# Sliding-window attention in a hybrid decoder step: where the scores of the next head group or sample row are issued on TensorE

## The chip, the cores and the metric

One core of one Trainium2 chip runs the whole kernel. The metric is device time in microseconds (us) of one execution, the median over a few executions. The engines are named as in the profile: PE is TensorE (PEld its weight loads), DVE is VectorE, ACT is ScalarE, POOL is GpSimd and SP is SyncE, which here only issues DMAs. Each engine works through its own list of instructions in order and waits on semaphores that the others raise.

## The reference

The kernel computes one layer of a decoder for a prompt of 256 tokens and for 8 sample rows of 8 tokens each. Everything is float32. One large input projection feeds three branches (sliding-window attention, retention, a gated spatial mix), an output projection joins them, and a mixture of 32 experts follows. The change touches the attention branch only:

```
def sink_attention(q, k, v, mask, sinks):
    s = jnp.einsum('bnqhgd,bnkhd->bnhgqk', q, k) * (HEAD_DIM ** -0.5)
    s = jnp.where(mask[None, :, None, None], s, -jnp.inf)
    m = jnp.maximum(jnp.max(s, axis=-1, keepdims=True), sink)
    p = jnp.exp(s - m)
    denom = jnp.sum(p, axis=-1, keepdims=True) + jnp.exp(sink - m)
    return jnp.einsum('bnhgqk,bnkhd->bnqhgd', (p / denom).astype(v.dtype), v)
```

There are 16 query heads in 4 groups (one key and value head each), heads are 64 wide, and the window is 128. The prompt is two tiles of 128 queries: the first sees 128 keys, the second 256. Each sample row sees 128 cached keys and the 64 new ones under a mask.

## The kernel before

The order of the work on each engine is written out by hand. In the attention stage TensorE runs, for prompt tile `t` (0, 1) and head group `g` (0 to 3), this round:

1. the scores `sc` of the group, 4 heads (L1317 to L1324; one PSUM bank for tile 0, two for tile 1);
2. for the first six rounds one unit of the modulation matrix, `modulation(6 + 4t + g)` (L1216), which has nothing to do with attention;
3. two pieces of the input projection, `project(2)` (L1264 for full token tiles, L1271 for the tile of 64 sample tokens);
4. a wait until the softmax of this group is done (`probs_ready`), then the transposes `pT` of the probabilities (L1334, recorded at the helper L1200);
5. a wait until ScalarE has copied `pT` out of PSUM (L611), then the value products `pv` (L1342).

The modulation and projection are there so that TensorE has work while VectorE and ScalarE compute the softmax. For the 8 sample rows the round is the same without the modulation, with one projection piece: scores (L1354, L1355), `project(1)`, transposes, a wait for the ScalarE copies (L618, L619), value products (L1369, L1370).

VectorE adds the mask to the scores as it takes them out of PSUM into the one buffer `probs` (L859, L866, L877), does its part of the softmax (L841 to L850), and copies the value products of a prompt group out (L872) before it takes the next scores. ScalarE does the exponentials (L598), takes the projection's pieces (L548), copies the transposes, and for the sample rows takes the value products too (L622).

Small results share three PSUM banks. The list `AUX` names every use of them in the order in which TensorE issues them; entry `n` has bank `5 + n % 3`. `aux_free(name)` makes TensorE wait until entry `n - 3` has been taken out of that bank, `aux_filled` makes a reader wait for an entry, and `aux_taken` waits until one has been read.

Weights of the projections come in units of 2 MB through three slots, issued by SyncE: unit `u` is loaded when unit `u - 3` has been used up (L330). The cached keys and values of the sample rows lie in two slots. GpSimd issues the load for row `b` (L385, L386) when the value products of row `b - 2` are done. After the last row the result is transposed back (`oback`, L1377). This releases further loads by GpSimd (L402 to L409), and TensorE does one more projection piece, then waits for a layer normalisation on VectorE (L928 to L930) before the products of L1390.

Of the kernel before, what the change touches and what calls it, by code (L numbers as in the profile page):

```python
# [24 lines left out]
P = 128  # L25
# [70 lines left out]
AUX += ["ada4", "ada5", "kT0", "kT1", "kT2"]  # L96
for _t in range(2):
    AUX += [f"qT{_t}{q}" for q in range(4)]
    for _g in range(KVH):
        AUX += [f"sc{_t}{_g}{k}" for k in range(_t + 1)]  # L100
        AUX += [f"ada{6 + 4 * _t + _g}"] if 4 * _t + _g < 6 else []
        AUX += [f"pT{_t}{_g}{k}" for k in range(_t + 1)] + [f"pv{_t}{_g}"]
AUX += ["qT20", "qT21"]
for _b in range(BATCH_S):
    AUX += [f"sc2{_b}", f"pT2{_b}", f"pv2{_b}"]
AUX += ["oback0", "oback1"]
AUX += [f"mix{t}{h}" for t in range(3) for h in range(2)]
for _t in range(2):
# [17 lines left out]
def build(nc, ctx, ins, outs):  # L126
# [159 lines left out]
    def aux_bank(name):  # L286
        return ps[:, AUX_FIRST + AUX_AT[name] % AUX_BANKS, :]
# [5 lines left out]
    def aux_taken(eng, name):  # L293

        n = AUX_AT[name]
        eng.wait_ge(aux_used[n % AUX_BANKS], n // AUX_BANKS + 1)
# [899 lines left out]
    def _(pe):  # L1196
        mm = nc.tensor.matmul

        def tr(out, in_, r, **kw):
            return nc.tensor.transpose(out, in_, ident[0:r, 0:r], **kw)  # L1200

        def aux_free(name):

            n = AUX_AT[name]
            if n >= AUX_BANKS:
                pe.wait_ge(aux_used[n % AUX_BANKS], n // AUX_BANKS)
# [104 lines left out]
        softmaxes = 0  # L1311
        for t in range(3):
            aux_taken(pe, f"kT{t}")
        for t in range(2):
            transpose_queries(t)
            for g in range(KVH):
                for k in range(t + 1):  # L1317
                    name = f"sc{t}{g}{k}"
                    aux_free(name)
                    n, width = (4, P) if t == 0 else (2, 2 * P)  # L1320
                    for m in range(n):
                        last = mm(aux_bank(name)[:, m * width:(m + 1) * width], qTa[0:64, 4 * g + n * k + m, :],  # L1322
                                  kTa[0:64, g, 0:width], start=True, stop=True)
                    last.then_inc(aux_ready, 1)  # L1324
                if 4 * t + g < 6:
                    modulation(6 + 4 * t + g)
                project(2)
                softmaxes += 1
                pe.wait_ge(probs_ready, softmaxes)
                for k in range(t + 1):  # L1330
                    name = f"pT{t}{g}{k}"
                    aux_free(name)
                    for h in range(GROUP):
                        last = tr(aux_bank(name)[:, h * P:h * P + P], probs[:, h, k * P:k * P + P], P)  # L1334
                    last.then_inc(aux_ready, 1)
                name = f"pv{t}{g}"
                aux_free(name)
                for k in range(t + 1):
                    aux_taken(pe, f"pT{t}{g}{k}")
                for h in range(GROUP):  # L1340
                    for k in range(t + 1):
                        last = mm(aux_bank(name)[:, h * HD:(h + 1) * HD], pT[:, k, h * P:h * P + P],  # L1342
                                  V[:, k, 256 + g * HD:256 + (g + 1) * HD], start=(k == 0), stop=(k == t))
                last.then_inc(aux_ready, 1)

        transpose_queries(2)
        for b in range(BATCH_S):
            name = f"sc2{b}"
            aux_free(name)
            pe.wait_ge(cache_in[b % 2], 32 * (b // 2 + 1))  # L1350
            keys = cache[0:64, b % 2, 0:512].rearrange("p (h r) -> p h r", h=KVH)
            for g in range(KVH):
                q = qTs[0:64, b, GROUP * g:GROUP * (g + 1), :].rearrange("p h t -> p (h t)")
                mm(aux_bank(name)[32 * g:32 * g + 32, 0:P], q, keys[:, g, :], start=True, stop=True, skip_group_check=True)  # L1354
                last = mm(aux_bank(name)[32 * g:32 * g + 32, P:192], q, kTa[0:64, g, SEQ:TOKENS], start=True, stop=True, skip_group_check=True)  # L1355
            last.then_inc(aux_ready, 1)
            project(1)
            softmaxes += 1
            pe.wait_ge(probs_ready, softmaxes)
            name = f"pT2{b}"  # L1360
            aux_free(name)
            tr(aux_bank(name)[:, 0:P], probs[:, 0, 0:P], P)
            tr(aux_bank(name)[0:64, P:2 * P], probs[:, 0, P:192], P).then_inc(aux_ready, 1)
            name = f"pv2{b}"
            aux_free(name)
            aux_taken(pe, f"pT2{b}")
            for g in range(KVH):
                out = aux_bank(name)[0:64, 32 * g:32 * g + 32]
                mm(out, cache[:, b % 2, 512 + g * HD:512 + (g + 1) * HD], pT[:, 0, 32 * g:32 * g + 32], start=True, stop=False)  # L1369
                last = mm(out, V[0:64, 2, 256 + g * HD:256 + (g + 1) * HD], pT[0:64, 1, 32 * g:32 * g + 32], start=False, stop=True)  # L1370
            last.then_inc(aux_ready, 1)
# [379 lines left out]
```

## Time and profile before

| | us |
|---|---|
| median of 3 runs | 1659.16 (1657.5 to 1659.64) |
| profiled execution, its own time | 1667.73 |
| span of the profiled execution (first to last instruction) | 1665.9 |
| PE busy in the span | 1566.5 (94%) |
| DVE busy | 483.0 (29%) |
| ACT busy | 318.4 (19%) |
| POOL busy | 97.6 (6%) |
| mean granted TensorE clock | 0.96 of full speed |

The attention stage runs from about 112 us to about 360 us of the span. What lies after 700 us is the loop over the experts.
### The profile page before, as it was taken

How to read it: one execution, taken by the hardware profiler on the slowest of the kernel's cores; microseconds unless marked ns; L12 is line 12 of the kernel's file. 1: busy time of each engine (PE TensorE's matmuls, PEld its weight loads, DVE VectorE, ACT ScalarE, POOL GpSimd, SP SyncE). 2: the span in 40 equal slices, each digit the busy share in tenths (PEclk: the TensorE clock that was granted, in tenths of full speed). 3: DMA queues.
4: the chain of work that ended last, by engine and by line, in shares of the span. 5: the costliest groups of instructions: out<-in, count | busy, mean ns of one | idle time of the engine just before them, and what ended most of it. 6: DMA issues, size and time to landing. Idle time of an engine off the chain costs nothing.

```text
span 1665.9 us, 20091 instructions
## 1 busy us (share of the span) xinstructions
PE 1566.5 (94%) x7989; PEld 670.2 (40%) x7990; DVE 483.0 (29%) x801; ACT 318.4 (19%) x582; POOL 97.6 (6%) x102
## 2 busy tenths in 40 slices
PE   5989899979999797999999999999999999999996
PEld 4455555545455455333333333333333333333332
DVE  2141222146234735122222222222222222222224
ACT  1123321111223222111111111111111111111110
POOL 0000000120222440000000000000000000000000
PEclk8989997899999896999999999999999999999999
DMA  9563531342232561899999999999693999999993
GB/s 361 180 253 111 222 123 58 126 139 74 98 133 76 183 228 51 319 428 428 429 428 429 429 429 428 428 428 428 247 410 161 412 425 429 429 428 428 429 429 138
DMA packets 38630, 492.00 MB, mean 295 GB/s; under 512 B 4800, under 2 KB 4928, under 8 KB 9792
## 3 DMA queue, kind: packets, MB, share of 16 engines
q1 hardware_dynamic: 34144, 477.27, 69.3%
q0 software_dynamic: 4448, 14.19, 3.0%
q8 instruction: 28, 0.46, 0.1%
q14 instruction: 10, 0.08, 0.0%
HBM read 487.12 MB, written 4.33 MB: 295 GB/s over the span
## 4 chain that ended last, share of the span: by engine, by line
PE 89%; DVE 4%; DMA 3%; ACT 2%; issue 1%; POOL 1%; SPq 0%; DVEq 0%; POOLq 0%
PE ps L1593 28%; PE ps L1264 17%; PE ps L1622 14%; PE ps L1542 6%; PE ps L1556 6%; PE ps L1271 5%; PE ps L1200 4%; DMA ring<-in_w_dense 2%; PE ps L1223 1%; PE ps L1216 1%; PE ps L1598 1%; PE ps L1322 1%; PE ps L1342 1%; ACT ring L548 1%; PE ps L1504 1%
## 5 line engine op out<-in xcount | busy, mean ns | idle before, releaser
L1593 PE MATMUL ps<-ring,arena 128*64 128x512 f32 x2176 | 481.1, 595 | 2.7 <-issue 2.7
L1264 PE MATMUL ps<-ring,xT 128*128 128x512 f32 x672 | 309.6, 618 | 3.0 <-DMA ring<-in_w_dense 2.3
L1593 PEld LDWEIGHTS ps<-ring,arena 128*64 128x64 f32 x2176 | 156.2, 137 | 309.4 <-issue 306.8
L1622 PE MATMUL ps<-ring,arena 128*64 128x512 f32 x1088 | 248.5, 598 | 0.0
L1178 DVE TENSOR_TENSOR U<-ps,U 128x1024 f32<-128x1024 f32 (+1 forms) x102 | 124.4, 1220 | 248.7 <-PE ps L1556 248.7
L1264 PEld LDWEIGHTS ps<-ring,xT 128*128 128x128 f32 x672 | 130.2, 198 | 162.8 <-issue 158.4
L1622 PEld LDWEIGHTS ps<-ring,arena 128*64 128x64 f32 x1088 | 71.9, 136 | 168.2 <-issue 142.4
L1556 PE MATMUL ps<-arena 64*128 64x512 f32 x420 | 119.6, 636 | 0.8 <-ACT arena L734 0.8
L1542 PE MATMUL ps<-T,arena 128*64 128x512 f32 (+1 forms) x420 | 105.7, 621 | 1.2 <-DVE arena L1068 1.2
L1169 DVE TENSOR_SCALAR arena<-ps 128x512 f32<-128x512 f32 x34 | 23.5, 692 | 217.4 <-PE ps L1598 217.4
L707 ACT ACTIVATE W<-ps 128x512 f32<-128x512 f32 x35 | 20.9, 597 | 339.8 <-PE ps L1542 339.8
L1271 PE MATMUL ps<-ring,xT 128*64 128x256 f32 x672 | 84.1, 407 | 0.0
L1167 DVE TENSOR_SCALAR arena<-ps 128x512 f32<-128x512 f32 x34 | 23.5, 692 | 188.4 <-PE ps L1598 188.4
L1271 PEld LDWEIGHTS ps<-ring,xT 128*64 128x64 f32 x672 | 49.5, 146 | 34.1 <-issue 14.2
L725 ACT ACTIVATE arena<-arena 128x512 f32<-128x512 f32 x34 | 21.4, 629 | 205.4 <-DVE arena L1167 205.4
L548 ACT ACTIVATE ring<-ps 128x512 f32<-128x512 f32 (+1 forms) x48 | 23.4, 488 | 190.6 <-PE ps L1264 160.1
L1542 PEld LDWEIGHTS ps<-T,arena 128*64 128x64 f32 (+1 forms) x420 | 24.3, 136 | 76.9 <-issue 76.9
L731 ACT ACTIVATE arena<-ps 128x320 f32<-128x320 f32 x34 | 14.9, 437 | 203.2 <-PE ps L1556 203.2
L1200 PEld LDWEIGHTS ps<-consts,arena 128*128 128x128 f32 (+2 forms) x321 | 35.1, 138 | 41.9 <-issue 41.6
L1200 PE MATMUL ps<-consts,arena 128*128 128x128 f32 (+2 forms) x321 | 48.5, 278 | 0.5 <-ACT arena L622 0.5
L1216 PE MATMUL ps<-ring 128*32 128x128 f32 x768 | 28.3, 311 | 18.3 <-DMA ring<-in_w_dense 18.3
L1556 PEld LDWEIGHTS ps<-arena 64*128 64x128 f32 x420 | 33.6, 189 | 29.6 <-issue 29.6
(266 smaller groups left out, 1056.8 us busy)
## 6 DMA issues: line engine op xcount, KB each, us to landing
ring<-in_w_moe SPq DMA_DIRECT2D x192, 2048.0 KB, 15.1
ring<-in_w_dense SPq DMA_DIRECT2D x33, 2048.0 KB, 8.1
V<-in_state POOLq DMA_DIRECT2D x6, 256.0 KB, 9.5
out_sample_retention<-V POOLq DMA_DIRECT2D x6, 256.0 KB, 4.0
R<-in_x_prompt SPq DMA_DIRECT2D x1, 1024.0 KB, 16.7
arena<-in_cache_kT POOLq DMA_DIRECT2D x8, 128.0 KB, 3.5
arena<-in_cache_v POOLq DMA_DIRECT2D x8, 128.0 KB, 3.5
arena<-in_b_gate POOLq DMA_DIRECT2D x4, 256.0 KB, 3.7
```

Source lines behind the costliest of these rows:

```text
L548: A(buf[0:ROWS[t], t, c0 + c:c0 + c + w], src, func).then_inc(z_used, 1)
L1167: X.tensor_scalar(g_cut, ps[:, 0, :], LIMIT, None, ALU.min).then_inc(g_cut_ready, 1)
L1169: X.tensor_scalar(u_cut, ps[:, 1, :], LIMIT, -LIMIT, ALU.min, ALU.max).then_inc(dve_step, 1)
L1178: X.tensor_tensor(both, ps[0:r, 6:8, :], both, ALU.add).then_inc(added, 1)
L1200: return nc.tensor.transpose(out, in_, ident[0:r, 0:r], **kw)
L1216: last = mm(aux_bank(name)[32 * j:32 * j + 32, 0:128], silu_c[:, k, :], wv[:, k, 128 * j:128 * j + 128], start=(k == 0), stop=(k == KD - 1 ...
L1264: last = mm(banks[t][0], xT[:, k, t * P:t * P + P], wv[:, k, :], start=(k == 0), stop=(k == KD - 1))
L1271: last = mm(banks[2 + a][0], xT[:, k, 2 * P:TOKENS], wv[:, k, 256 * a:256 * a + 256], start=(k == 0), stop=(k == KD - 1), skip_group_check ...
L1542: last = mm(ps[64 * a:64 * a + 64, 3, :], pick[0:r, t, :], T[0:r, t, HALF * a:HALF * a + HALF], start=(t == 0), stop=(t == 2), skip_group_ ...
L1556: last = mm(ps[:, first + a, :], gateT[64 * a:64 * a + 64, t * P:(t + 1) * P], y_blk[64 * a:64 * a + 64, :], start=True, stop=True)
L1593: last = mm(ps[64 * a:64 * a + 64, half, :], xgT[:, k, j % 2, :], wv[:, k, HALF * a:HALF * a + HALF], start=(j % 2 == 0 and k == 0), stop= ...
L1622: last = mm(ps[64 * a:64 * a + 64, 2, :], actT[:, k, j - 4, :], wv[:, k, HALF * a:HALF * a + HALF], start=(j == 4 and k == 0), stop=(j == ...
```

## The change

TensorE issues the scores one step earlier. Only those of group 0 of each prompt tile and of sample row 0 stay ahead of their round. The scores of group `g + 1` (for `g` below 3) are issued after the transposes of group `g` and before its value products, those of sample row `b + 1` after the transposes of row `b` and before its value products. The list `AUX` has the same 150 entries in the new order, so which entry lies three before another changes at some places. The other engines run the same instructions in the same order.

```
+    AUX += [f"sc{_t}0{k}" for k in range(_t + 1)]
     for _g in range(KVH):
-        AUX += [f"sc{_t}{_g}{k}" for k in range(_t + 1)]
...
+        AUX += [f"sc{_t}{_g + 1}{k}" for k in range(_t + 1)] if _g + 1 < KVH else []
...
+        def scores(t, g):
+            for k in range(t + 1):
+                name = f"sc{t}{g}{k}"
+                aux_free(name)
+                n, width = (4, P) if t == 0 else (2, 2 * P)
+                for m in range(n):
+                    last = mm(aux_bank(name)[:, m * width:(m + 1) * width], qTa[0:64, 4 * g + n * k + m, :],
+                              kTa[0:64, g, 0:width], start=True, stop=True)
+                last.then_inc(aux_ready, 1)
+
         for t in range(2):
             transpose_queries(t)
+            scores(t, 0)
             for g in range(KVH):
-                for k in range(t + 1):
-                    name = f"sc{t}{g}{k}"
-                    aux_free(name)
-                    n, width = (4, P) if t == 0 else (2, 2 * P)
-                    for m in range(n):
-                        last = mm(aux_bank(name)[:, m * width:(m + 1) * width], qTa[0:64, 4 * g + n * k + m, :],
-                                  kTa[0:64, g, 0:width], start=True, stop=True)
-                    last.then_inc(aux_ready, 1)
                 if 4 * t + g < 6:
                     modulation(6 + 4 * t + g)
                 project(2)
...
                         last = tr(aux_bank(name)[:, h * P:h * P + P], probs[:, h, k * P:k * P + P], P)
                     last.then_inc(aux_ready, 1)
+                if g + 1 < KVH:
+                    scores(t, g + 1)
                 name = f"pv{t}{g}"
                 aux_free(name)
...
-        transpose_queries(2)
-        for b in range(BATCH_S):
+        def sample_scores(b):
             name = f"sc2{b}"
             aux_free(name)
             pe.wait_ge(cache_in[b % 2], 32 * (b // 2 + 1))
...
             last.then_inc(aux_ready, 1)
+
+        transpose_queries(2)
+        sample_scores(0)
+        for b in range(BATCH_S):
             project(1)
             softmaxes += 1
             pe.wait_ge(probs_ready, softmaxes)
...
             tr(aux_bank(name)[0:64, P:2 * P], probs[:, 0, P:192], P).then_inc(aux_ready, 1)
+            if b + 1 < BATCH_S:
+                sample_scores(b + 1)
             name = f"pv2{b}"
             aux_free(name)
             aux_taken(pe, f"pT2{b}")
```

How TensorE's list stands at two places follows. The first is tile 1, from the transposes of group 0 (L1200, two sets of four) to the modulation unit of group 1 (L1216); the scores are L1322, the value products L1342, and in brackets are the semaphores waited for (`aux_used0` to `aux_used2` tell that a shared bank was read). Before:

```order
L1200 MATMUL ps<-consts,arena 128x128 [waits aux_used0]
L1200 MATMUL ps<-consts,arena 128x128 x3
L1342 MATMUL ps<-V,arena 128x64 [waits aux_used0,aux_used2,aux_used1]
L1342 MATMUL ps<-V,arena 128x64 x7
L1322 MATMUL ps<-arena,U 128x256 [waits aux_used2]
L1322 MATMUL ps<-arena,U 128x256
L1322 MATMUL ps<-arena,U 128x256 [waits aux_used0]
L1322 MATMUL ps<-arena,U 128x256
L1216 MATMUL ps<-ring 32x128 [waits aux_used1,unit_in0]
```

The same place in the changed kernel, whose lines are numbered anew (L1202 transposes, L1323 scores, L1350 value products, L1218 modulation):

```order
L1202 MATMUL ps<-consts,arena 128x128 [waits aux_used0]
L1202 MATMUL ps<-consts,arena 128x128 x3
L1323 MATMUL ps<-arena,U 128x256 [waits aux_used1]
L1323 MATMUL ps<-arena,U 128x256
L1323 MATMUL ps<-arena,U 128x256 [waits aux_used2]
L1323 MATMUL ps<-arena,U 128x256
L1350 MATMUL ps<-V,arena 128x64 [waits aux_used0,aux_used2]
L1350 MATMUL ps<-V,arena 128x64 x7
L1218 MATMUL ps<-ring 32x128 [waits aux_used1,unit_in0]
```

The scores have moved ahead of the value products. The modulation unit waits for `aux_used1` in both, but the entry three before it was `pv10` (the value products of group 0) and is now `sc110` (the first scores of group 1).

The second place is TensorE at sample rows 0 and 1: transposes (L1200), value products (L1369, L1370), scores (L1354, L1355), projection (L1271). Before, from the second transpose of row 0, with the middle of the value products and of the scores left out:

```order
L1200 MATMUL ps<-consts,arena 64x128
L1369 MATMUL ps<-arena 64x32
L1370 MATMUL ps<-arena,V 64x32
...
L1354 MATMUL ps<-arena,U 32x128
L1355 MATMUL ps<-arena,U 32x64
...
L1271 MATMUL ps<-ring,xT 64x256 x16
```

In the changed kernel the scores are L1361 and L1362, the value products L1382 and L1383:

```order
L1202 MATMUL ps<-consts,arena 64x128
L1361 MATMUL ps<-arena,U 32x128
L1362 MATMUL ps<-arena,U 32x64
...
L1382 MATMUL ps<-arena 64x32
L1383 MATMUL ps<-arena,V 64x32
...
L1273 MATMUL ps<-ring,xT 64x256 x16
```

The eight score matmuls of row 1 stand between the transposes and the eight value products of row 0, and the projection piece now follows the value products directly.

## Rows read from the trace of the kernel before

**Rows 1.** The page: TensorE in the whole span.
```profile
PE 1566.5 (94%) x7989; PEld 670.2 (40%) x7990; DVE 483.0 (29%) x801; ACT 318.4 (19%) x582; POOL 97.6 (6%) x102
```

**Rows 2.** Waits from 100 to 420 us: us in total, times, longest.
```profile
PE ps L1390 <- DVE ring L930: 9.9, 1, 9.9
...
PE ps L1369 <- ACT arena L619: 7.6, 8, 1.1
PE ps L1342 <- ACT arena L611: 7.2, 8, 1.1
...
PE ps L1264 <- DMA ring<-in_w_dense: 2.3, 1, 2.3
```

**Rows 3.** Stretches: length, busy of PE, PEld, DVE, ACT, POOL, PEclk, DMA share, GB/s.
```profile
188.00:272.80 84.80, 78.86 (x469) 47.63 (x469) 21.36 (x43) 28.03 (x66) 0.00 (x0) 0.92 0.32 124
272.80:359.40 86.60, 78.59 (x448) 43.65 (x449) 21.57 (x85) 15.42 (x59) 6.53 (x12) 0.86 0.23 78
```

**Rows 4.** Timeline, PE, tile 0: start us, us, instructions, idle before.
```profile
133.43 1.08 PE L1342 MATMUL ps<-V,arena 128*128 128x64 f32 x8 [0.83 <-ACT arena L611]
134.44 1.16 PE L1322 MATMUL ps<-arena,U 64*128 64x128 f32 x8
135.52 1.95 PE L1216 MATMUL ps<-ring 128*32 128x128 f32 x64
...
165.72 1.08 PE L1342 MATMUL ps<-V,arena 128*128 128x64 f32 x8 [1.00 <-ACT arena L611]
...
172.05 14.00 PE L1264 MATMUL ps<-ring,xT 128*128 128x512 f32 x32 [2.29 <-DMA ring<-in_w_dense]
```

**Rows 5.** Timeline, PE, tile 1: value products of groups 0 and 1, and what follows.
```profile
207.79 1.97 PE L1342 MATMUL ps<-V,arena 128*128 128x64 f32 x16 [0.88 <-ACT arena L611]
209.69 1.99 PE L1322 MATMUL ps<-arena,U 64*128 64x256 f32 x8
...
226.31 1.97 PE L1342 MATMUL ps<-V,arena 128*128 128x64 f32 x16 [1.06 <-ACT arena L611]
228.21 3.78 PE L1322 MATMUL ps<-arena,U 64*128 64x256 f32 x8
231.92 15.55 PE L1264 MATMUL ps<-ring,xT 128*128 128x512 f32 x32
```

**Rows 6.** Timeline, DVE, after the value products of tile 1, group 0.
```profile
209.87 0.42 DVE L872 COPY T<-ps 128x256 f32<-128x256 f32 x1 [9.87 <-PE ps L1342]
210.92 0.69 DVE L866 TENSOR_TENSOR arena<-ps,consts 128x512 f32<-128x512 f32 x1 [0.63 <-PE ps L1322]
```

**Rows 7.** Timeline, PE, sample rows 2 to 4.
```profile
298.30 9.62 PE L1264 MATMUL ps<-ring,xT 128*128 128x512 f32 x16
...
311.31 7.13 PE L1264 MATMUL ps<-ring,xT 128*128 128x512 f32 x16
318.28 0.38 PE L1200 MATMUL ps<-consts,arena 128*128 128x128 f32 x2
319.54 0.27 PE L1369 MATMUL ps<-arena 128*64 128x32 f32 x2 [0.88 <-ACT arena L619]
...
321.35 0.44 PE L1354 MATMUL ps<-arena,U 64*32 64x128 f32 x8
...
321.83 3.67 PE L1271 MATMUL ps<-ring,xT 128*64 128x256 f32 x32
```

**Rows 8.** Timeline, POOL: the load of the cache for sample row 5.
```profile
322.24 0.57 POOL L386 DMA_DIRECT2D arena<-in_cache_v  x1
```

**Rows 9.** DMA issues from 327 to 333 us, row 6: KB, us to landing.
```profile
arena<-in_cache_v POOLq DMA_DIRECT2D x1, 128.0 KB, 4.8
```

**Rows 10.** DMA issues from 320 to 326 us, row 5.
```profile
arena<-in_cache_v POOLq DMA_DIRECT2D x1, 128.0 KB, 2.5
```

**Rows 11.** Timeline, POOL and DVE, after the last sample row.
```profile
360.76 0.54 POOL L402 DMA_DIRECT2D arena<-in_gm_ln_g  x1 [20.03 <-PE ps L1200]
...
371.05 2.86 DVE L928 TENSOR_SCALAR ring<-ring,stat 128x1024 f32<-128x1024 f32 x1 [2.52 <-DMA arena<-in_mixT_s]
```

More of the change, by code:

```diff
@@ L98 @@
     AUX += [f"qT{_t}{q}" for q in range(4)]
+    AUX += [f"sc{_t}0{k}" for k in range(_t + 1)]
     for _g in range(KVH):
-        AUX += [f"sc{_t}{_g}{k}" for k in range(_t + 1)]
         AUX += [f"ada{6 + 4 * _t + _g}"] if 4 * _t + _g < 6 else []
-        AUX += [f"pT{_t}{_g}{k}" for k in range(_t + 1)] + [f"pv{_t}{_g}"]
-AUX += ["qT20", "qT21"]
+        AUX += [f"pT{_t}{_g}{k}" for k in range(_t + 1)]
+        AUX += [f"sc{_t}{_g + 1}{k}" for k in range(_t + 1)] if _g + 1 < KVH else []
+        AUX += [f"pv{_t}{_g}"]
+AUX += ["qT20", "qT21", "sc20"]
 for _b in range(BATCH_S):
-    AUX += [f"sc2{_b}", f"pT2{_b}", f"pv2{_b}"]
+    AUX += [f"pT2{_b}"] + ([f"sc2{_b + 1}"] if _b + 1 < BATCH_S else []) + [f"pv2{_b}"]
 AUX += ["oback0", "oback1"]
```

## Prediction

> **What bounds the kernel now.** I read the page first. It shows TensorE busy for 1566.5 of 1665.9 us [rows 1], with no other engine above 29%, so a gap that closes on TensorE is worth its full length unless something later waits anyway. Next I read the table of waits for the stretch of the attention, since the change acts only there. Two of its lines are what the change aims at: TensorE stands still before the prompt's value products for 7.2 us in 8 waits and before the sample rows' for 7.6 us in 8 waits, both times until ScalarE has copied the transposed probabilities out of PSUM [rows 2]. That is 14.8 us, the ceiling for what can be filled. Two more lines of that table could swallow a gain: one wait for a weight unit (2.3 us) and one of 9.9 us for the layer normalisation behind the attention [rows 2]. Last I read the table of stretches for the clock: 0.92 in tile 1 and 0.86 in the sample rows [rows 3]. With levels of 1.00 and 0.50, a mean of 0.92 over 84.8 us is 13.6 us at half speed and 0.86 over 86.6 us is 24.2 us, together some 38 us. So the clock is a second cost of this stage, larger than the gaps.
>
> **The change part by part.** Nothing is added or removed: the same matmuls run, and 3 + 3 prompt groups and 7 sample rows have their scores moved. Group 3 of each tile and sample row 7 have no following scores, so 3 of the 16 gaps stay.
>
> *Tile 0.* The value products start at 133.43 after 0.83 us of idling, so the transposes ended at about 132.60, and the scores take 134.44 to 135.52, 1.08 us [rows 4]. Put into the gap, 1.08 us of scores cover all of 0.83 us. ScalarE needs the same time for its copy, and the value products find it done. Groups 0 and 1 give 0.83 us each (one row stands for both, with the same number). Group 2 has a gap of 1.00 us, but the projection after it waits 2.29 us for a weight unit [rows 4]. That unit was released by an earlier piece of projection, ahead of this gap, so its arrival does not move with it: TensorE comes 1.00 us earlier and waits 3.29 us. Tile 0 gives 2 x 0.83 = 1.66 us. If the unit did arrive earlier by 1.0 us it would be 2.66; if the gaps were not filled, 0.
>
> *Tile 1.* The gaps before groups 0, 1 and 2 are 0.88, 1.06 and again 0.88 us (the third row reads like the first), and the scores take 1.99 us at full clock [rows 5], so the gaps are covered as well: 2.82 us. The second half of these scores goes to a bank that ScalarE must have emptied of the first transposes. It has about 1 us for that (the first half of the scores), which is longer than the whole gap in two of the three, so I cost this at nothing; if it failed, it would be at most 0.1 us in each. Against it stands a new wait. The modulation unit of group 1 shares its bank with the first scores of group 1, which VectorE takes only after it has copied the value products of group 0. Before, the scores lay between and hid this. Now the matmuls of the unit come straight after the value products. VectorE started its copy 0.11 us after the value products ended (207.79 + 1.97 = 209.76, copy at 209.87), copied for 0.42 us, and needs 0.69 us to take the scores [rows 6]. With about 0.2 us for the two hand-overs that is 0.11 + 0.42 + 0.69 + 0.2 = 1.4 us of new idling. Queued behind the waiting matmul is all of TensorE's list (the unit, then two projection pieces), so it counts in full. From below it is bounded by nothing if VectorE were ahead, which its own order excludes; from above by the two steps plus the longest hand-over in the rows, 0.63 us: 1.9 us. The other modulation units have entries three before them that are read long before. Tile 1 gives 2.82 - 1.4 = 1.4 us (0.9 to 2.8).
>
> *Sample rows.* The scores take 321.35 to 321.83, 0.48 us, and the gap is 0.88 us after a full projection piece [rows 7] and up to 1.06 us after a short one [rows 2]. ScalarE's copies set the start of the value products, so 0.48 us of work slips under the gap and 0.40 us of idling is left: 7 x 0.48 = 3.4 us. The moved scores also wait for their cached keys earlier than before. The tightest place is after a short projection piece: cache row 5 is issued at 322.24 and lands 2.5 us later, at 324.7 [rows 8, 10]. The scores of row 5 would now want it one short piece (321.83 to about 325.4) and two transposes after the value products of row 3, less the 0.48 us of scores that left, at about 325.2. That leaves 0.5 us. A load that shares the DMA engines with a weight unit took 4.8 us [rows 9]; this one did so ahead of a full piece of 7.13 us, which covers it. I cost it at nothing; at 4.8 us in both short rows it would be 2 x 1.8 = 3.6 us. VectorE's softmax for the next row can start during the value products and only gains cover.
>
> *Behind the attention.* The 9.9 us wait is not a fixed date. The last transposes back release GpSimd's loads at 360.76, and VectorE waits 2.52 us for one of them before the normalisation [rows 11]. All of this hangs on TensorE and moves with it, so the gain passes through. The expert loop follows TensorE too.
>
> Sum of what is direct: 1.66 + 1.4 + 3.4 = 6.4 us.
>
> *The clock.* The half-speed stretches begin around the thin places of a round: the gap, value products that are short and narrow, and scores. What one costs is read from tile 1: the scores after group 1 took 3.78 us instead of 1.99, and the two projection pieces 15.55 instead of 14.00 [rows 4, 5], 3.3 us in all; in a sample row, 9.62 instead of 7.13 for the projection piece [rows 7], 2.5 us. Half of the 38 us is the ceiling, 19 us. The change shortens the thin place of a sample row from transposes to projection (318.28 to 321.83, 3.55 us) by 0.48 us, some 14%, and in tile 1 it takes a gap out and puts one in. I take a tenth of 17 us, 1.7 us, as the likeliest. It could be anything from a gain of four stretches (13 us) to a loss of two (6.6 us), since a slight shift decides whether a thin place is answered by a lower clock: among the sample rows with the same pattern, row 2 ran at half speed and row 3 did not [rows 7].
>
> The Trainium skill ("TensorE: Matmul & The Clock Gate", HAM oscillation) says that a hardware monitor gates the clock by how busy the array has recently been, and under its second failure mode that micro-idles between groups of matmuls, repeated in each iteration, make the clock swing. By that rule this change would return more than the gaps themselves, up to most of the 19 us. The same page says that the monitor runs free of the kernel, by which the outcome may differ from one execution to the next. The trace agrees that half speed follows the thin places, but rows 2 and 3 of the samples show that the same pattern goes either way.
>
> Total: 6.4 + 1.7 = 8.1 us. The profiled execution took 1667.73 us, 1.8 us more than its span of 1665.9; minus 8.1 that is 1659.6. The median of the runs is 8.6 us under the profiled execution, so I expect 1659.16 - 8.1 = 1651.1 us.
>
> **The rivals.**
> - *The clock gives back more.* Three half-speed stretches fewer, at 3.3 us: 6.4 + 9.9 = 16.3, so 1642.9 us. For it: 38 us at half speed lie right at the places changed. Against it: the thin value products of the sample rows, 1.8 us of a 3.55 us place, stay as they are.
> - *The clock takes it back.* One or two stretches more, 3.3 to 6.6 us: 1656 to 1659.4 us. For it: the new wait of 1.4 us follows directly on value products, and the wait for the weight unit grows to 3.3 us. Against it: everywhere else TensorE becomes denser.
> - *The gain is absorbed.* If the normalisation behind the attention were held by something that does not move with TensorE, or weight units came no earlier, the 6.4 us would reappear as a longer wait there: 1658 to 1659. Against it stands what released those waits [rows 11].
> - *The cache loads become the bound (slower).* Value products of row b release the load for row b + 2, which the moved scores of row b + 2 now want before the value products of row b + 1. If a load took 8 us, the two short rows would wait (8 - 3.5) = 4.5 us each and five long ones about 1 us each: 14 us of waits minus 6.4, 1667 us. It decides from about 3.5 us of landing in short rows and 7 in long ones; the rows show 2.5 and 4.8.
> - *The change does not do what it says* would be TensorE still idling in the gaps because the scores wait for their own bank. The entries three before are read in time by the same rows, so I give this no chance of its own beyond the absorbed case.
>
> **How the numbers follow.** Forecast 0.52 (1647 to 1655 by its own bounds); clock gives more 0.22; clock takes back 0.15; absorbed 0.06; slower 0.05. From 1642.5 to 1658.5 all but the end of the second case and most of the last two are inside. About 0.2% (3.3 us) is what a measurement of this kernel can tell from no change. Faster by more than that: 0.52 + 0.22 + a third of 0.15 = 0.79. Same: two thirds of 0.15 and the absorbed case, 0.16. Slower: 0.05.
>
> **What the profile after would show.** The waits before the prompt's value products fall from 7.2 us to about 1.9 us (two groups 3), those before the sample rows' from 7.6 to about 4.2 us. A new wait of about 1.4 us stands before one modulation unit, released by VectorE's mask addition. The weight unit's wait reads about 3.3 us. The 9.9 us wait stays as it is. No wait for the cache appears before the scores. Total time at half speed in the attention stays between 20 and 45 us. The prediction is wrong if the stage from 112 us to the last sample row shortens by less than 4 us or more than 16, and the clock's row would then say whether it was the gaps or the clock.

## The result and the profile after

| | before | changed kernel |
|---|---|---|
| median, us (6 runs each) | 1659.4 (1656.3 to 1660.98) | 1650.24 (1646.91 to 1652.91) |
| ratio, 95% interval | 1 | 0.9945 (0.993 to 0.9961) |
| profiled execution, us | 1667.73 | 1647.98 |
| span, us | 1665.9 | 1646.1 |
| mean granted clock of the span | 0.960 | 0.968 |

The change saves 9.2 us, and 1651.1 was predicted. A second set of 7 runs of the changed kernel gave 1651.06 us and the ratio 0.9949 (0.9931 to 0.9967). The two profiled executions differ by 19.75 us, twice the difference of the medians, because that of before is 8 us above its median and that of after 2 us below. Two executions far outside the rest, one of before at 1710.15 us and one of before_dense at 3199.51 us, are left out of all ratios. In what follows the waits are read from the profiles, and the clock's share from all runs.

The page of the changed kernel, to be set beside [rows 1]: TensorE does the same matmuls in 11.2 us less busy time.
```profile
PE 1555.3 (94%) x7989; PEld 667.3 (41%) x7990; DVE 483.4 (29%) x801; ACT 317.7 (19%) x582; POOL 97.8 (6%) x102
```

The table of waits of the changed kernel, 100 to 420 us, in us in total, times, and the longest (L1382 sample value products, L1350 prompt value products, L1218 modulation, L1266 projection, L1403 the products behind the layer normalisation):
```profile
PE ps L1403 <- DVE ring L932: 6.8, 1, 6.8
...
PE ps L1382 <- ACT arena L621: 4.2, 8, 1.1
PE ps L1266 <- DMA ring<-in_w_dense: 4.0, 1, 4.0
...
PE ps L1350 <- ACT arena L613: 1.7, 2, 0.9
PE ps L1218 <- DVE arena L868: 1.4, 1, 1.4
```
Against [rows 2], the waits before the value products fell from 7.2 to 1.7 us and from 7.6 to 4.2 us. The wait for the weight unit grew from 2.3 to 4.0 us and one new wait of 1.4 us is there. In sum 7.2 + 7.6 + 2.3 = 17.1 us became 1.7 + 4.2 + 4.0 + 1.4 = 11.3 us: 5.8 us less waiting ahead of the layer normalisation.

The timeline of TensorE in the changed kernel at three places (start us, us, instructions, idle before): tile 0 group 0, tile 0 group 3, and tile 1 from the scores of group 1 to its modulation unit:
```profile
131.18 1.16 PE L1323 MATMUL ps<-arena,U 64*128 64x128 f32 x8
132.26 1.10 PE L1350 MATMUL ps<-V,arena 128*128 128x64 f32 x8
133.30 1.96 PE L1218 MATMUL ps<-ring 128*32 128x128 f32 x64
...
169.61 15.70 PE L1266 MATMUL ps<-ring,xT 128*128 128x512 f32 x32 [3.99 <-DMA ring<-in_w_dense]
...
206.10 1.99 PE L1323 MATMUL ps<-arena,U 64*128 64x256 f32 x8
208.02 2.00 PE L1350 MATMUL ps<-V,arena 128*128 128x64 f32 x16
211.42 3.29 PE L1218 MATMUL ps<-ring 128*32 128x128 f32 x64 [1.40 <-DVE arena L868]
```
The bracket of 0.83 us before the value products in [rows 4] has gone, and so has the 0.88 us in [rows 5]: the scores stand there now. The last row is the new wait. VectorE shows what TensorE waits for, as against [rows 6] where it waited for the scores itself:
```profile
210.12 0.42 DVE L874 COPY T<-ps 128x256 f32<-128x256 f32 x1 [10.86 <-PE ps L1350]
210.58 1.42 DVE L868 TENSOR_TENSOR arena<-ps,consts 128x512 f32<-128x512 f32 x2
```
Copy and first mask addition now follow each other without a gap, and TensorE continues when the first addition is done. In a full sample row 0.39 us of the 0.88 us of [rows 7] are left:
```profile
301.87 0.44 PE L1361 MATMUL ps<-arena,U 64*32 64x128 f32 x8
...
302.82 0.27 PE L1382 MATMUL ps<-arena 128*64 128x32 f32 x2 [0.39 <-ACT arena L621]
```

The stretches of the changed kernel (length, busy of PE, PEld, DVE, ACT, POOL, then PEclk, DMA share, GB/s): tile 0, tile 1, sample rows.
```profile
111.70:187.50 75.80, 70.95 (x497) 41.12 (x498) 14.07 (x39) 24.20 (x58) 0.00 (x0) 0.95 0.48 190
187.50:265.40 77.90, 73.38 (x466) 45.46 (x466) 21.36 (x43) 27.93 (x66) 0.00 (x0) 0.98 0.35 135
265.40:339.90 74.50, 69.86 (x455) 39.87 (x456) 21.88 (x87) 14.67 (x59) 6.56 (x12) 0.97 0.27 95
```
Beside [rows 3] the clock rose from 0.92 to 0.98 in tile 1 and from 0.86 to 0.97 in the sample rows. Tile 1 is 84.80 - 77.90 = 6.9 us shorter. The last window ends 0.6 us too late to be set beside that of before, since the transposes back begin at 339.28; up to there the sample rows take 73.9 us, 12.7 us less than before. Both are far more than the waits that went. In this pair of executions the clock is most of it. What other executions say of that follows behind before_dense2.

### The profile page after: what moved, and what is told of

The parts are those of the page before. It is cut to its first block, busy times and chain, and to the rows that moved or that the text cites. A ratio compares the mean times of both kernels' runs of the same rounds, so it can differ in the third digit from the quotient of the medians.

```text
span 1646.1 us, 20091 instructions
## 1 busy us (share of the span) xinstructions
PE 1555.3 (94%) x7989; PEld 667.3 (41%) x7990; DVE 483.4 (29%) x801; ACT 317.7 (19%) x582; POOL 97.8 (6%) x102
## 4 chain that ended last, share of the span: by engine, by line
PE 89%; DVE 4%; DMA 3%; ACT 2%; issue 1%; POOL 1%; SPq 0%; DVEq 0%; POOLq 0%
PE ps L1606 29%; PE ps L1266 17%; PE ps L1635 15%; PE ps L1555 6%; PE ps L1569 6%; PE ps L1202 5%; PE ps L1273 4%; DMA ring<-in_w_dense 2%; PE ps L1225 1%; PE ps L1218 1%; PE ps L1611 1%; PE ps L1323 1%; PE ps L1350 1%; ACT ring L550 1%; PE ps L1517 1%
## 5 line engine op out<-in xcount | busy, mean ns | idle before, releaser
L1266 PE MATMUL ps<-ring,xT 128*128 128x512 f32 x672 | 307.0, 613 | 4.7 <-DMA ring<-in_w_dense 4.0
L1266 PEld LDWEIGHTS ps<-ring,xT 128*128 128x128 f32 x672 | 129.2, 196 | 162.1 <-issue 156.0
L1273 PE MATMUL ps<-ring,xT 128*64 128x256 f32 x672 | 77.2, 382 | 0.0
L1202 PEld LDWEIGHTS ps<-consts,arena 128*128 128x128 f32 (+2 forms) x321 | 36.0, 141 | 41.8 <-issue 41.8
L1202 PE MATMUL ps<-consts,arena 128*128 128x128 f32 (+2 forms) x321 | 49.3, 282 | 0.5 <-ACT arena L624 0.5
L1218 PE MATMUL ps<-ring 128*32 128x128 f32 x768 | 29.2, 317 | 19.5 <-DMA ring<-in_w_dense 18.1
```

The lines of the kernel that those rows point to most:

```text
L1218: last = mm(aux_bank(name)[32 * j:32 * j + 32, 0:128], silu_c[:, k, :], wv[:, k, 128 * j:128 * j + 128], start=(k == 0), stop=(k == KD - 1 ...
L1266: last = mm(banks[t][0], xT[:, k, t * P:t * P + P], wv[:, k, :], start=(k == 0), stop=(k == KD - 1))
L1273: last = mm(banks[2 + a][0], xT[:, k, 2 * P:TOKENS], wv[:, k, 256 * a:256 * a + 256], start=(k == 0), stop=(k == KD - 1), skip_group_check ...
```

## The experiments

All times are medians; ratios are to the kernel before, run on the same chip, where its own medians were 1659.2 to 1659.9 us. Over the runs of all kernels (148), a run with 1 us more at half speed than its kernel's mean (2 x (1 - mean clock) x span) took 0.34 us longer. By the same formula the half-speed time of a run was, on average, 113 us in before (57 runs), 106 us in the changed kernel (13 runs).

**prompt_only** takes the sample rows back to the old order (the entries of `AUX` go back with them):
```
-        sample_scores(0)
         for b in range(BATCH_S):
+            sample_scores(b)
             project(1)
...
-            if b + 1 < BATCH_S:
-                sample_scores(b + 1)
```

> Only the prompt's scores are moved (3 groups of each tile); the sample rows keep their order. Theory A (the direct terms add up, the clock gives a little): tile 0 saves 1.7 us, tile 1 saves 1.4 us after the new wait of 1.4 us, so 3.1 us under before, with the clock 3 to 5 us under. Theory B (most of the gain is the clock in tile 1, where the half-speed stretches after groups 1 and 2 vanish): 6 to 9 us under before, and the stretch from the first scores to the transposes for the sample rows has at most one half-speed stretch.

Measured: 1652.62 us, 0.995 (0.9935 to 0.9966), half-speed time 107 us. Its waits are exactly those of the two kernels it is made of: 7.6 us before the sample value products, 1.7 us before the prompt's, 4.0 and 1.4 us for the weight unit and the modulation. The 0.5% are 8 us (5.6 to 10.8 by the interval), in the range of theory B and above that of theory A. Tile 1 has one half-speed stretch left, behind the new wait.

**sample_only** is the opposite, the prompt in its old order (`scores(t, g)` at the head of the round).

> Only the scores of the sample rows are moved; the prompt keeps its order. Theory A: 7 x 0.48 = 3.4 us direct, with the clock 3.5 to 5.5 us under before. Theory B (the clock in the sample rows gives as much as the gaps): 6 to 9 us under before and fewer half-speed stretches between the sample rows. The waits before the sample value products read about 4.2 us in total in either case, those before the prompt's value products stay at 7.2 us.

Measured: 1650.93 us, 0.9941 (0.9926 to 0.9956), half-speed time 104 us. Its waits are 4.2 us before the sample value products, 7.2 us before the prompt's, 1.9 us for the weight unit. This too lies in the range of theory B and above that of A. Both parts alone gained 0.5% and 0.6%, and the two together 0.55%. The waits do add up: (7.2 + 2.3 - 1.7 - 1.4 - 4.0) + (7.6 + 2.3 - 4.2 - 1.9) = 2.4 + 3.8 = 6.2, against 5.8 in the changed kernel. What does not add up is the rest. The half-speed time fell by 6 us, by 9 us, and by 7 us with both. Each interval is some 5 us wide, which is a part of the answer; beyond that, why two parts regain no more of the clock than one is open.

**after_again** is the changed kernel beside these two.

> The changed kernel once more, beside the others on the same chip. Theory A and B: 8 to 10 us under before. If prompt_only and sample_only add up to this, the two parts are independent; if the clock is a lottery of where the stretches fall, its sum differs from theirs by 3 us or more and another profile of it shows its half-speed stretches at other places than the first.

Measured: 1651.06 us, 0.9949 (0.9931 to 0.9967). Its profile had the same waits as the first. Its runs lay between 1646.65 us (the profiled one) and 1655.86 us, at mean clocks of 0.972 and 0.965. Only the first has a trace, so that the slower one had the same waits is not shown, but over all kernels the spread goes with the clock (the 0.34 us above). The gains of the two parts add up to 18 us, some 10 us more than this kernel's, as the expectation has it for a clock that is a lottery; but the half-speed stretches did not move in tile 1 and in the sample rows (0.98 and 0.97 again), only in tile 0 (0.98 instead of 0.95).

**before_dense** and **before_dense2** are one kernel: the old order, with scores computed a second time in each gap, into the bank that the value products overwrite. Shown for the prompt:
```
                 name = f"pv{t}{g}"
                 aux_free(name)
+                for m in range(3):
+                    mm(aux_bank(name)[:, m * P:(m + 1) * P], qTa[0:64, 4 * g + m, :], kTa[0:64, g, 0:P], start=True, stop=True)
```

> The order of before, but TensorE computes some scores a second time inside each of the 16 gaps (3 products of 128 columns in the prompt, the 8 small ones of a sample row), into the bank that the value products overwrite next. This adds work and moves nothing, so nothing is saved directly. Theory A (the moved work is the gain, the clock is a side effect of 1 to 2 us): within 2 us of before. Theory B (a gap that is filled keeps the clock up, whatever fills it): 4 to 8 us under before, with fewer half-speed stretches in the attention. Rival C (the longer thin place costs clock): 3 us or more over before.

> before_dense once more, for its profile. In it the waits before the value products have shrunk to what the second copies of the scores leave (0.1 us or less in a prompt group, 0.4 to 0.6 us in a sample row), the waits on the weight unit and before the layer normalisation are those of before, and there are fewer than the 38 us at half speed that the attention of before had from tile 1 on. Theory B (whatever fills a gap keeps the clock up): 15 to 25 us there and 3 us under before. Theory A (only the moved work helps): 30 us or more.

Measured: 1656.38 us, 0.9976 (0.9963 to 0.9989), and again 1657.0 us, 0.9986 (0.9969 to 1.0003). The profile is that of before_dense2. Its waits, 100 to 420 us (L1396 behind the normalisation, L1375 sample value products, L1264 the weight unit, L1344 the prompt's value products):
```profile
PE ps L1396 <- DVE ring L930: 9.3, 1, 9.3
...
PE ps L1375 <- ACT arena L619: 3.0, 8, 0.5
...
PE ps L1264 <- DMA ring<-in_w_dense: 2.8, 1, 2.8
...
PE ps L1344 <- ACT arena L611: 0.2, 1, 0.2
```
And its stretches, tile 1 and the sample rows:
```profile
187.30:265.30 78.00, 75.80 (x493) 47.49 (x492) 21.36 (x43) 27.72 (x66) 0.00 (x0) 1.00 0.35 135
265.30:345.90 80.60, 76.87 (x588) 44.43 (x589) 21.87 (x87) 15.65 (x60) 6.54 (x12) 0.94 0.25 87
```
TensorE does more work here and nothing has moved, yet the kernel is 2 to 4 us faster, with 101 and 106 us at half speed in its runs against 113. The first gain stands at the edge of theory B's range (4 to 8 us), the second between that and theory A's (within 2 us), with an interval that just reaches 1; the times alone do not decide. The sample rows have 0.06 x 2 x 80.6 = 10 us at half speed and tile 1 none, less than the 15 to 25 us expected.

**The same stretches in other profiles.** The single profile of before is a weak measure of the clock, but other kernels hold the same stretch in the same order. Tile 1, from its first scores to those of the sample rows: the old order in before, sample_only and cache_late_before; the old order with filled gaps in before_dense2; the new order in the changed kernel and prompt_only; and the new order without the wait of 1.4 us in after_mid, which follows below.
```profile
191.52:272.79 81.27, 76.62 (x448) 45.80 (x449) 20.93 (x42) 25.39 (x62) 0.00 (x0) 0.91 0.33 130
196.09:274.04 77.95, 73.30 (x448) 44.07 (x449) 20.94 (x42) 25.27 (x62) 0.00 (x0) 0.96 0.35 135
192.64:270.59 77.95, 73.30 (x448) 44.09 (x449) 20.94 (x42) 25.28 (x62) 0.00 (x0) 0.96 0.35 135
190.99:265.61 74.62, 73.41 (x473) 45.53 (x473) 20.93 (x42) 25.29 (x62) 0.00 (x0) 1.00 0.36 141
190.78:265.40 74.62, 71.39 (x448) 43.88 (x449) 20.93 (x42) 25.28 (x62) 0.00 (x0) 0.98 0.36 141
193.45:268.07 74.62, 71.39 (x448) 43.81 (x449) 20.93 (x42) 25.28 (x62) 0.00 (x0) 0.98 0.36 141
195.63:267.02 71.39, 69.56 (x449) 42.43 (x450) 20.82 (x42) 25.28 (x62) 0.00 (x0) 1.00 0.38 148
```
The sample rows, from their first scores to the transposes back: the old order in prompt_only, the old order with filled gaps in before_dense2, the new order in the changed kernel and sample_only.
```profile
268.07:346.82 78.75, 70.72 (x449) 39.66 (x449) 19.98 (x82) 15.43 (x59) 6.54 (x12) 0.96 0.25 85
265.61:345.27 79.66, 76.24 (x576) 43.77 (x577) 21.53 (x85) 15.44 (x59) 6.54 (x12) 0.94 0.25 85
265.40:339.28 73.88, 69.25 (x448) 39.25 (x449) 21.62 (x86) 14.67 (x59) 6.56 (x12) 0.97 0.27 92
274.04:347.64 73.60, 68.97 (x448) 39.21 (x449) 21.38 (x85) 14.65 (x59) 6.54 (x12) 0.98 0.27 91
```
In tile 1 two of the three profiles of the old order agree on 77.95 us at 0.96. In all three the clock falls at the same place, behind the gap of 1.06 us and the value products of group 1: the scores there take 3.3 to 3.8 us instead of 1.99, and the two projection pieces 15.6 to 16.0 us instead of 14.0. With the gaps filled by useless matmuls it does not fall there, and tile 1 takes 74.62 us at 1.00. So in tile 1 theory B holds, with one trace against three: filling the gaps is worth 3.3 us even where nobody reads what fills them. The new order takes 74.62 us in all four of its traces (after_again and cache_late_after too), 3.3 us less than the old one: 2.82 - 1.40 = 1.4 us of waits and 1.9 us of clock.

In the sample rows the new order takes 73.6 to 73.9 us against 78.75 us in prompt_only, 4.9 us less: 3.4 us of waits and 1.5 us of clock. There filling the gaps with useless matmuls brought nothing (79.66 us at 0.94), so that whatever fills a gap keeps the clock up is not shown for them. The old order does not always have the clock of 0.86 that before had there in its profile. Tile 0 scatters most: from its first scores to those of tile 1 it takes 77.7 to 82.5 us in three profiles of the old order and 77.0 to 81.6 us in five of the new one.

**after_mid** removes the new wait of 1.4 us:
```
-                if 4 * t + g < 6:
+                if 4 * t + g < 5:
                     modulation(6 + 4 * t + g)
-                project(2)
+                project(1)
+                if 4 * t + g == 5:
+                    modulation(11)
+                project(1)
```

> The changed kernel, with the modulation unit of tile 1, group 1 issued between the two projection pieces of its round instead of ahead of them, so that VectorE has 3.6 to 7 us to take the scores out of the bank that the unit waits for. Theory A: the wait of 1.40 us before the modulation unit is gone, and 1.4 us is saved against the changed kernel, some 10 us against before. Rival: the bias that VectorE adds from this unit comes later in its softmax and delays the transposes, so the 1.4 us return as a wait for the probabilities and the time is that of the changed kernel. Rival D (clock): the difference lies within 3 us either way and goes with the time at half speed.

Measured: 1647.4 us, 0.9922 (0.9904 to 0.994), some 3 us under the changed kernel. The timeline of TensorE at the place:
```profile
212.87 2.00 PE L1353 MATMUL ps<-V,arena 128*128 128x64 f32 x16
214.71 7.08 PE L1266 MATMUL ps<-ring,xT 128*128 128x512 f32 x16
221.72 1.95 PE L1218 MATMUL ps<-ring 128*32 128x128 f32 x64
```
The wait is gone, nothing took its place, and the unit runs in 1.95 us where it took 3.29 us after the wait: the idling had also cost the clock there, 1.3 us. Theory A holds. The interval overlaps that of the changed kernel, so the 3 us are not a firm number by the times; tile 1 by itself became 74.62 - 71.39 = 3.2 us shorter. The clock does not answer this wait every time: the unit took 3.2 to 3.6 us behind it in the four traces of the new order, but 1.96 us in that of sample_fill.

**weights** goes further: the six modulation units are spread over rounds 0, 1, 2 and 4, 5, 7 and the weight units ordered to match.
```
-               ("ada", 9), ("proj", CV0), ("ada", 10), ("proj", CV1), ("ada", 11)]
+               ("proj", CV0), ("ada", 9), ("proj", CV1), ("ada", 10), ("proj", RQ), ("ada", 11)]
...
+MOD_AT = {0: 6, 1: 7, 2: 8, 4: 9, 5: 10, 7: 11}
```

> The changed kernel with the six modulation units spread over rounds 0, 1, 2 of tile 0 and 0, 1, 3 of tile 1, and their weight units loaded in that order, so that the unit for the projection in tile 0, group 3 is released earlier; the modulation of rounds 1 and 3 of tile 1 stands between the projection pieces. The same matmuls run. Theory A: the wait of 4.0 us for the weight unit and the wait of 1.4 us before the modulation unit both go: 5.4 us under the changed kernel, some 14 us under before. Rival: the weight loads are the pace of this stretch and the wait turns up before another unit: no more than 2 us under the changed kernel.

Measured: 1640.77 us, 0.988 (0.9858 to 0.9903). In its table of waits both the weight unit's 4.0 us and the modulation's 1.4 us have no row, and in the timeline the projection of tile 0, group 3 follows the value products:
```profile
162.88 1.10 PE L1355 MATMUL ps<-V,arena 128*128 128x64 f32 x8
163.82 13.95 PE L1267 MATMUL ps<-ring,xT 128*128 128x512 f32 x32
```
The gain of 10 us over the changed kernel is more than the 5.4 us of waits; the half-speed time of its 4 runs was 94 us against 106, which at 0.34 to 0.5 us each is 4 to 6 us. The loads are not the pace of this stretch.

**sample_fill** adds the first step of the next projection piece in each sample row, ahead of the value products (`fill(1)` issues one of its 8 steps, and the next `project` the rest):
```
             if b + 1 < BATCH_S:
                 sample_scores(b + 1)
+            fill(1)
```

> The changed kernel, and in each of the 8 sample rows the first of the 8 steps of the next projection piece (0.86 us, or 0.45 us in a short piece) is issued after the moved scores, ahead of the value products. Theory A: the 4.2 us that TensorE still stands before the sample value products go, 4.2 us under the changed kernel, some 13 us under before; value products come up to 0.5 us later, which nobody waits for. Theory B: denser thin places also cut the time at half speed, 1 to 4 us more. Rival: later value products hold back ScalarE's exponentials and the cache loads, and the gain is under 2 us.

Measured: 1644.38 us, 0.9916 (0.9896 to 0.9937). The 4.2 us of waiting became 0.2 us, and some 6 us went from the time. Its interval and that of the changed kernel still overlap a little.

**best** is weights and sample_fill together with the steps in the other gaps.

> weights and sample_fill together, and a projection step also in the gaps of group 3 of both tiles (0.83 and 0.88 us) and while ScalarE copies the transposed queries of tile 1 and of the sample rows (1.29 and 0.95 us). Theory A: 5.4 + 4.2 + 1.7 + 2.2 = 13.5 us under the changed kernel, some 22 us under before, about 1638 us. If the gains overlap (the weight unit sets the date of tile 0's end), 3 us less. Theory B: with the half-speed time cut as well, down to 1633 us.

Measured: 1633.56 us, 0.9844 (0.9822 to 0.9866), 26 us under before. Of the waits that these orders touch, this is left in the prompt, before the first scores of its two tiles and before the value products:
```profile
PE ps L1361 <- ACT U L592: 1.3, 2, 1.0
...
PE ps L1394 <- ACT arena L614: 0.2, 1, 0.2
```
Before the sample value products 0.2 us are left too, and the wait for the layer normalisation stays at 7.1 us. It is the fastest of all that ran, with the same matmuls as before in another order.

**cache_late_after** and **cache_late_before** test the slower rival. The cached keys of each row from 2 on are loaded twice in a chain, so that the data counts some 2.7 us later:
```
+            if b >= 2:
+                pool.dma_start(cache[0:64, b % 2, 0:512]..., ins["cache_kT"][b]).then_inc(cache_late, 16)
+                pool.wait_ge(cache_late, 16 * (b - 1))
```

> The changed kernel, with the cached keys of each row from 2 on loaded twice, the second load (which counts) only after the first has landed, so that keys and values land about 3 us later (the first load's issue of 0.5 us and 2.4 to 2.5 us to landing). Theory (the slack of the moved scores is about 0.5 us in a short row and 3 to 4 us in a long one): the scores of rows 2 and 5, wanted after the short pieces of rows 1 and 4, wait about 2.5 us each, the long rows 0 to 1 us: 5 us over the changed kernel, some 4 us under before. Rival (there is more slack than I read): the time of the changed kernel. The prediction's slower rival needs only a longer landing still.

> The kernel before with the same double load. Its scores want the cached keys a full round later, after the value products of the row between, so a landing 3 us later is still in time in every row. Theory: the time of before within 2 us, and no wait before the scores. If this one slows down as well, the load costs by something other than the date of the scores.

Measured: 1665.6 us, 1.0049 (1.003 to 1.0067), for the changed kernel and 1664.47 us, 1.0021 (0.9993 to 1.0048), for the kernel before. The changed kernel is now slower than before without the double load. Its two waits stand where they were expected, before the scores of rows 2 and 5:
```profile
288.65 0.68 PE L1364 MATMUL ps<-arena,U 64*32 64x128 f32 x8 [6.62 <-DMA arena<-in_cache_v]
...
324.44 0.67 PE L1364 MATMUL ps<-arena,U 64*32 64x128 f32 x8 [5.60 <-DMA arena<-in_cache_v]
```
But they are 6.6 and 5.6 us long, not 2.5 us. The GpSimd queue of that kernel at row 2, and the DMA issues from 281 to 284 us with their KB and us to landing, say why:
```profile
278.36 0.52 POOL L388 DMA_DIRECT2D arena<-in_cache_kT  x1 [169.67 <-PE ps L1386]
281.14 0.52 POOL L390 DMA_DIRECT2D arena<-in_cache_kT  x1 [2.26 <-DMA arena<-in_cache_kT]
281.65 0.57 POOL L391 DMA_DIRECT2D arena<-in_cache_v  x1
```
```profile
ring<-in_w_dense SPq DMA_DIRECT2D x1, 2048.0 KB, 8.0
arena<-in_cache_kT POOLq DMA_DIRECT2D x1, 128.0 KB, 2.5
arena<-in_cache_v POOLq DMA_DIRECT2D x1, 128.0 KB, 6.9
```
The short projection piece ends at 281.6, and its end releases a weight unit of 2 MB. The late load of the values starts at that moment and takes 6.9 us instead of 2.4 us; at row 5 it takes 6.0 us, with a weight unit issued 0.2 us behind it. In the changed kernel without the double load the values of rows 2 and 5 land 0.7 and 0.8 us before their scores begin (278.51 + 2.4 against 281.60, 305.52 + 2.3 against 308.60), so 2.7 us alone would have given waits of some 2 us. The kernel before, which was to be unharmed, met the same collision at row 2 (keys 6.4 us, values 8.6 us) with a wait of 5.8 us; that there would be no wait was wrong. Its time is not clear of that of before, since the interval takes in 1. With the load this late the two orders take about the same time.

## Why the prediction was right

- **The gaps.** The terms of the prompt were 0.83 us twice and 2.82 us; the waits there fell by 5.5 us with the third of tile 0 (1.00 us), which adds up to 5.48 us. The sample rows' 3.4 us were measured as 7.6 - 4.2 = 3.4 us. The second half of tile 1's scores never waited for its bank.
- **The new wait** was priced at 1.4 us and is 1.40 us. What the price left out is that it pulled the clock down for the unit behind it, 1.3 us more in the profiled execution; without it tile 1 is 3.2 us shorter (after_mid).
- **The weight unit** was to absorb group 2's 1.00 us and read 3.3 us. It reads 4.0 us in every profile with the moved prompt scores. The unit arrived 8.5 us after its release instead of 7.9 us (169.61 - 161.07, 172.05 - 164.16). The next load is issued 1 us earlier in relation to it, which may slow it, but no run shows that. The wait also varies where the prompt's scores stand in their old place, 1.9 us in sample_only and 2.8 us in before_dense2.
- **The direct sum** was 6.4 us and the waits give 5.8 us, the difference being this unit.
- **The clock** was the mis-sized term, 1.7 us. The medians leave 9.2 - 5.8 = 3.4 us for it, the stretches give 1.9 us in tile 1 and 1.5 us in the sample rows, and 7 us less at half speed at a price between 0.34 us (the scatter of the runs) and 0.5 us (at half speed half of the time is lost) give 2.4 to 3.5 us. That 1.7 us came as near as it did is luck: the tenth had no source, and the 17 us of which it was taken stand nowhere in the working, where the ceiling is 19 us. The error of the clock and that of the weight unit went opposite ways, and the total is off by 1.1 us. The mechanism named in the prediction is what before_dense2 shows by itself in tile 1. The Trainium skill's rule that recurring micro-idles between groups of matmuls make the clock swing ("TensorE: Matmul & The Clock Gate", second failure mode) holds here in tile 1: 1.00 instead of 0.96 once the gaps were filled with work that nobody reads. In the sample rows the trace does not bear it out (0.94 with filled gaps, 0.96 without). What the rule does not give is the size, and the up to 19 us that I read from one profile of before were an overestimate, since that execution (1667.73 us) was above every one of the 57 timed runs of before used here.
- **The end of the attention.** I said that the 9.9 us wait would stay. It reads 6.8 us, and 6.5 to 9.3 us in the other kernels. The transposes and the projection piece ahead of it ran in part at half speed in the changed kernel (9.04 us instead of 7.13 us), so TensorE came later to a date set elsewhere. The gain did pass through this wait, as the argument from [rows 11] had it: the products behind the normalisation start 377.42 - 359.40 = 18.0 us after the transposes back before, and 356.94 - 339.28 = 17.7 us after them in the changed kernel.
- **The slower rival** was rightly kept at 5%. Its place was right (no wait in the changed kernel, two with 2.7 us more). Its slack was worked out in two ways that do not agree, 0.5 us over a landing of 2.5 us in one place and a landing of 3.5 us in the other; the trace gives 3.1 us (281.60 - 278.51). Its price was far off: past the point where it decides, the load meets the weight unit.
- **What would have made it wrong.** By my own list the stage should have shortened by 4 to 16 us with 20 to 45 us at half speed. In the profiled pair it shortened by 247.6 - 227.6 = 20.0 us (111.81 to 359.40, 111.73 to 339.28), and tile 1 and the sample rows, which I had counted at 38 us at half speed, have 8 us. By both marks the profile says that the prediction failed, while the medians say that it held. The marks were drawn from one profile of before that has more time at half speed than sample_only has in the old order of tile 1 and prompt_only in that of the sample rows: a single profile on each side is no measure of a clock that differs from run to run.

## What to carry to other kernels

When an engine waits a short time for its partner's copy in every round, move independent work of the next round into that gap, and then follow each buffer of the rotation anew: the entry that a later step must see emptied may now be one that is read late. On TensorE a short gap in a thin part of the program can cost more than its length, because the clock answers it: here 3.3 us behind a gap of 1.06 us. A run's mean clock beside its time helps to separate the two, and a kernel that fills the gaps with useless work measures the second part alone. Where one profile gives the clock of a stretch, look for the same stretch in the same order in the profiles of the other kernels. A load that lands just in time should be placed by what is issued next to it: a big transfer released at about the same moment made 2.4 us into 6.0 to 8.6 us here.

## What the hardware showed that was not expected

Useless matmuls made the kernel faster (0.9976 and 0.9986 with 16 gaps filled), and in tile 1 a gap of 1.06 us was answered by a lower clock in three profiles of three. A 128 KB load took 6.0 to 8.6 us instead of 2.4 us when a 2 MB load started within 0.4 us of it. Seven executions of the changed kernel differed by 9 us at mean granted clocks from 0.964 to 0.972, and 29 of before by 18 us (1649.49 us at 0.975, 1667.33 us at 0.962).
